# Expert layers: five split buffers, slabs split before the gather, zeros written during the layer before, and 8 KB weight rows with gate and up products of 256 columns

## The reference, cut to what matters

```python
def moe_ffn(x, w_router, b_router, w_gate, w_up, w_down):
    ...
    s = jax.nn.sigmoid((xt @ w_router).astype(jnp.float32))
    biased = s + b_router.astype(jnp.float32)
    grp_score = lax.top_k(biased.reshape(n, N_EXPERT_GROUPS, EXPERTS_PER_GROUP), TOP_K)[0].sum(-1)
    grp = jnp.argmax(grp_score, axis=-1)
    ...
    h = jax.nn.silu(jnp.einsum('nd,edf->nef', xt, w_gate)) * jnp.einsum('nd,edf->nef', xt, w_up)
    h = h * gate[:, :, None].astype(h.dtype)
    return jnp.einsum('nef,efd->nd', h, w_down).reshape(B, S, D)
```

## Time and profile before

| | us |
|---|---|
| median of three runs | 2281.39 (2280.94 to 2286.85) |
| profiled execution, its own time | 2280.86 |
| its span in the trace | 2279.1 |
| first expert layer, from its first POOL instruction to the last down product's start | 1159.80 to 1442.96 |
| second expert layer, likewise | 1962.79 to 2245.17 |
| PE, DVE, ACT, POOL busy over the span | 90%, 61%, 42%, 7% |

### The profile page before, as it was taken

How to read it: one execution, slowest core, us unless ns; L and a number is a source line. 1 busy time by engine, 2 the same in 40 slices (tenths; PEclk the granted TensorE clock), 3 DMA queues, 4 the chain that set the end, 5 groups by cost and what they waited for, 6 DMA issues and landing times. The chain is left out here.

```text
span 2279.1 us, 29889 instructions
## 1 busy us (share of the span) xinstructions
PE 2046.0 (90%) x11912; PEld 1732.2 (76%) x11912; DVE 1383.8 (61%) x1962; ACT 949.9 (42%) x1399; POOL 151.4 (7%) x209
## 2 busy tenths in 40 slices
PE   5999988969999898999979999699968887799995
PEld 5888878869999786776758888478957666688784
DVE  7864545545555454533468999745036675689896
ACT  5653335221000001623447777421125552477773
POOL 3442000000000000000020001000000000010010
PEclk9999998989999999999989999899879999799998
DMA  7433112214232223221249999432420002199993
GB/s 212 109 73 95 56 56 94 74 36 123 76 110 76 73 75 98 79 89 38 74 150 363 388 390 383 169 89 93 117 76 1 1 1 73 40 363 386 386 385 145
DMA packets 162200, 325.53 MB, mean 143 GB/s; under 512 B 30176, under 2 KB 98464, under 8 KB 161936
## 3 DMA queue, kind: packets, MB, share of 16 engines
q1 hardware_dynamic: 133872, 282.92, 35.4%
q0 software_dynamic: 11792, 32.33, 4.4%
q10 hardware_dynamic: 16400, 8.39, 1.5%
HBM read 299.41 MB, written 18.94 MB: 140 GB/s over the span
## 5 line engine op out<-in xcount | busy, mean ns | idle before, releaser
L2277 PE MATMUL ps<-m_ws,m_xbT 128*128 128x512 f32 x1344 | 317.8, 392 | 1.6 <-DVE m_ws L2515 1.6
L2277 PEld LDWEIGHTS ps<-m_ws,m_xbT 128*128 128x128 f32 x1344 | 254.0, 189 | 54.9 <-DVE m_ws L2515 1.8
L2515 DVE TENSOR_TENSOR m_ws<-ring,m_ws 128x2048 fp32r<-128x2048 f32 x112 | 255.8, 2290 | 38.2 <-ACT m_ws L2355 31.6
L1630 PE MATMUL ps<-ffT,ff_ws 128*128 128x264 f32 (+1 forms) x1056 | 241.7, 324 | 4.4 <-DVE ff_ws L433 4.4
L2355 ACT CAST m_ws<-ring 128x2048 fp32r<-128x2048 f32 x112 | 213.2, 1909 | 74.5 <-PE ps L2277 38.6
L1630 PEld LDWEIGHTS ps<-ffT,ff_ws 128*128 128x128 f32 x1056 | 176.9, 190 | 20.2 <-DVE ff_ws L433 4.5
L2319 PE MATMUL ps<-m_ws,m_hT 128*128 128x512 f32 x672 | 170.6, 404 | 0.0
L1630 PE MATMUL ps<-ffT_lo,ff_ws 128*128 128x264 f32 (+1 forms) x528 | 170.3, 323 | 0.0
L2319 PEld LDWEIGHTS ps<-m_ws,m_hT 128*128 128x128 f32 x672 | 124.4, 192 | 24.7
L2512 DVE TENSOR_TENSOR m_ws<-ring,m_ws 128x2048 fp32r<-128x2048 f32 x56 | 128.2, 2290 | 12.9 <-ACT m_ws L2353 12.3
L460 PE MATMUL ps<-fd_ws,fd_xs 128*128 128x512 f32 x528 | 121.9, 394 | 6.7 <-DVE fd_xs L433 6.7
(11 more groups left out here) (540 smaller groups left out, 4295.0 us busy)
## 6 DMA issues: line engine op xcount, KB each, us to landing
ring<-in_moe_w_gate SPq DMA_DIRECT2D x112, 512.0 KB
ring<-in_moe_w_up SPq DMA_DIRECT2D x112, 512.0 KB
ring<-in_moe_w_down SPq DMA_DIRECT2D x56, 1024.0 KB
ring<-in_w_up SPq DMA_DIRECT2D x22, 1024.0 KB
ring<-in_w_in SPq DMA_DIRECT2D x16, 1024.0 KB
ring<-in_gla_w_in SPq DMA_DIRECT2D x12, 1024.0 KB
ring<-in_w_down SPq DMA_DIRECT2D x11, 1024.0 KB
ring<-in_nsa_w_in SPq DMA_DIRECT2D x10, 1024.0 KB
```

The source lines that it names most:

```text
L1630: ins = nc.tensor.matmul(ps[:, bank, 0:b - a], w[j][:, k, s * P:(s + 1) * P], x[l][:, k, a:b], start=(k == 0 and j == l), stop=(k == KD - ...
L2277: ins = nc.tensor.matmul(ps[:, it % 2, :], xbT[:, blk % 2, a, 4 * half + k, :].bitcast(F32R), v[b][:, k, :], start=(half == 0 and k == 0 a ...
L2515: ins = V.tensor_tensor(o, x.rearrange("p (j k w) -> p j k w", k=4, j=2), x0, ALU.subtract)
```

## The change

1. `SPLITS` becomes 5. Room for the fifth buffer is made by laying `rows` over `xT`. `rh` and `rl` move to buffers 3 and 4.
2. Slab 2 is therefore rounded by ACT ahead of the copies to `xbT`, and DVE splits slab 0 ahead of the router's ranking, slabs 1 and 2 where slabs 0 and 1 were, and 3 and 4 where 2 and 3 were.
3. POOL writes the zeros at the end of `gla_project`, from `xT`, for blocks 2 to 6 of `x_slots` (before: 0 to 6), `y_slots` and `g_slots`; ACT waits for them at the start of the expert layer.
4. A gate slab holds all of one expert's gate weights and an up slab all of its up weights. Each of the 128 partitions receives one run of 8 KB (before: two runs of 4 KB from two tensors). Down slabs are laid out as (p k) and not (k p), which is also a run of 8 KB; the transposes of `hb` take every second column to match. Gate and up become 48 matmuls with 256 columns, first all of gate, then all of up.

```diff
-SPLITS = 4
+SPLITS = 5
...
                 if down:
                     units[u][2] = self.W.add((slab_view(2, D), lambda expert=expert: expert("moe_w_down_2")
-                                              .rearrange("o (k p) w -> p (o k) w", p=P)))
+                                              .rearrange("o (p k) w -> p (o k) w", p=P)))
                     continue
-                for half in range(2):
-                    units[u][half] = self.W.add(*[
-                        (lambda s, j=j: s[:, 1024 * j:1024 * j + 1024],
-                         lambda name=name, half=half, expert=expert: expert(name)
-                         .rearrange("o (p k) w -> p o (k w)", p=P)[:, 0, 1024 * half:1024 * half + 1024])
-                        for j, name in enumerate(("moe_w_gate_2", "moe_w_up_2"))])
+                for j, name in enumerate(("moe_w_gate_2", "moe_w_up_2")):
+                    units[u][j] = self.W.add((lambda s: s, lambda name=name, expert=expert: expert(name)
+                                              .rearrange("o (p k) w -> p o (k w)", p=P)[:, 0, :]))
         return units
...
+                pool.wait_ge(o_done, N)
+                zero = m["xT"][:, 2:4].rearrange("p a c -> p (a c)")
+                nc.gpsimd.memset(m["xT"][:, 2:6], 0.0).then_inc(zeroed, 1)
+                pool.wait_ge(zeroed, 1)
+                for blk in range(2, NB):
+                    pool.dma_start(self.x_slots[P * blk:P * (blk + 1), :], zero).then_inc(self.zeros_in, 16)
+                pool.dma_start(self.y_slots[P * (NB - 2):P * NB, :].rearrange("(b p) d -> p b d", p=P),
+                               m["xT"][:, 2:6].rearrange("p (b a) c -> p b (a c)", b=2)).then_inc(self.zeros_in, 16)
+                pool.dma_start(self.g_slots.rearrange("(b p) e -> p b e", p=P), zero[:, 0:NB * EG].rearrange("p (b e) -> p b e", e=EG))\
+                    .then_inc(self.zeros_in, 16)
...
-            rows = sb(ctx, tag + "_rows", [P, TT, D])
+            rows = xT[:].rearrange("p k c -> p (k c)").rearrange("p (t d) -> p t d", t=TT)
...
-            rh, rl = (ws[:, 2 + y].rearrange("p a (t c) -> p (a t) c", t=2) for y in range(2))
+            rh, rl = (ws[:, 3 + y].rearrange("p a (t c) -> p (a t) c", t=2) for y in range(2))
...
-            n_sent = 16 * (2 * TT + (NB + 3 if first else 0))
+            n_sent = 16 * 2 * TT
...
                         for half in range(2):
                             q = at[units[it][half]]
                             pe.wait_ge(lo_done, q + 1)
-                            v = [slab_view(4, 512)(part(q, y)) for y in range(2)]
-                            for k in range(4):
-                                if it == 0:
-                                    pe.wait_ge(xp_out, 4 * half + k + 1)
+                            v = [slab_view(KD, 256)(part(q, y)) for y in range(2)]
+                            for k in range(KD):
+                                if it == 0 and half == 0:
+                                    pe.wait_ge(xp_out, k + 1)
                                 for a, b in ((0, 0), (0, 1), (1, 0)):
-                                    ins = nc.tensor.matmul(ps[:, it % 2, :], xbT[:, blk % 2, a, 4 * half + k, :].bitcast(F32R),
-                                                           v[b][:, k, :], start=(half == 0 and k == 0 and a == b),
-                                                           stop=(half == 1 and k == 3 and a == 1))
+                                    ins = nc.tensor.matmul(ps[:, it % 2, 256 * half:256 * half + 256], xbT[:, blk % 2, a, k, :].bitcast(F32R),
+                                                           v[b][:, k, :], start=(k == 0 and a == b), stop=(k == KD - 1 and a == 1))
                             ins.then_inc(slab_read, 1)
...
                         for k in range(2):
-                            ins = nc.tensor.transpose(ps[:, 2, P * k:P * (k + 1)], hb[:, u % 2, P * k:P * (k + 1)], self.ident[:])
+                            y = hb[:, u % 2].rearrange("p (q k) -> p k q", k=2)[:, k, :]
+                            ins = nc.tensor.transpose(ps[:, 2, P * k:P * (k + 1)], y, self.ident[:])
                         ins.then_inc(t_done, 1)
...
+                if first:
+                    act.wait_ge(self.zeros_in, 16 * NB)
...
                     x = W.slot(slabs[q])
-                    if down[q]:
-                        nc.scalar.copy(part(q, 0), x).then_inc(hi_done, 1)
-                    else:
-                        nc.scalar.copy(part(q, 0).rearrange("p (k j w) -> p j k w", k=4, j=2),
-                                       x.rearrange("p (j k w) -> p j k w", k=4, j=2)).then_inc(hi_done, 1)
+                    nc.scalar.copy(part(q, 0), x).then_inc(hi_done, 1)
...
                 nc.scalar.activation(s[:], ps[:, 4, 0:TT * NE], ACT.Sigmoid).then_inc(s_out, 1)
                 round_x(2)
                 round_x(3)
+                hi(2)
                 act.preload_act_table(ACT.Silu)
                 for k in range(KD):
                     act.wait_ge(xp_done, k + 1)
                     nc.scalar.copy(xbT[:, :, :, k, :].rearrange("p b a c -> p a b c").bitcast(F32R),
                                    ps[:, xbank[k], :].rearrange("p (a b c) -> p a b c", a=2, b=2)).then_inc(xp_out, 1)
-                hi(2)
                 hi(3)
+                hi(4)
...
-                if first:
-                    nc.gpsimd.memset(xb[:, 0, :], 0.0).then_inc(zeroed, 1)
-                    pool.wait_ge(zeroed, 1)
-                    for blk in range(NB):
-                        pool.dma_start(self.x_slots[P * blk:P * (blk + 1), :], xb[:, 0, 0:D]).then_inc(sent, 16)
-                    for blk in range(LAST, NB):
-                        pool.dma_start(self.y_slots[P * blk:P * (blk + 1), :], xb[:, 0, 0:D]).then_inc(sent, 16)
-                    pool.dma_start(self.g_slots.rearrange("(b p) e -> p b e", p=P), xb[:, 0, 0:NB * EG].rearrange("p (b e) -> p b e", e=EG))\
-                        .then_inc(sent, 16)
-                    pool.wait_ge(sent, 16 * (NB + 3))
                 pool.wait_ge(slot_done, 1)
...
                     x = W.slot(slabs[q])
-                    if down[q]:
-                        ins = V.tensor_tensor(part(q, 1), x, ws[:, q % SPLITS, 0], ALU.subtract)
-                    else:
-                        o, x0 = (y.rearrange("p (k j w) -> p j k w", k=4, j=2) for y in (part(q, 1), ws[:, q % SPLITS, 0]))
-                        ins = V.tensor_tensor(o, x.rearrange("p (j k w) -> p j k w", k=4, j=2), x0, ALU.subtract)
+                    ins = V.tensor_tensor(part(q, 1), x, ws[:, q % SPLITS, 0], ALU.subtract)
...
                 rest_x(0)
                 rest_x(1)
+                lo(0)
                 dve.wait_ge(loaded, 16 * len(loads))
                 dve.wait_ge(s_out, 1)
...
                     V.tensor_scalar(onehot[:, t].bitcast(F32R), slots, slotf[:, t:t + 1], None, ALU.is_equal).then_inc(hot, 1)
                 V.tensor_copy(slot[:], slotf[:]).then_inc(slot_done, 1)
-                lo(0)
                 lo(1)
+                lo(2)
...
                 V.tensor_copy(gid[:], gidf[:]).then_inc(gid_done, 1)
-                lo(2)
                 lo(3)
+                lo(4)
```

More of the change, by code:

```diff
@@ L1818, in gla_project @@
             ybank = (0, 4, 6, 2)
-            centred = self.sem("gl_centred")
+            centred, zeroed = self.sems("gl", "centred", "zeroed")
+            self.zeros_in = self.sem("zeros_in")
             self.n_ln += 1
@@ L2196, in moe_stage @@
             NQ = len(slabs)
-            down = [n in {u[2] for u in units} for n in slabs]
             block = ctx.enter_context(nc.Block())
```

## The result

The changed kernel took **2296.32 us** (median of 6 runs, 2295.77 to 2298.45), the kernel before 2282.64 us in the same comparison: ratio 1.006, 95% interval 1.0047 to 1.0073. It is 0.6% slower.

A forecast was written before the change was run, and what follows sets the result against it. PE was taken to bound the kernel, with DMA close behind. The terms 14.7 + 3.2 - 7 + 6 = +16.9 on the profiled 2280.86 gave 2297.8; with the median 0.5 above, 2298 us, range 2279 to 2314.

The forecast's parts named there:

- Passes: Gate and up in all 56 units: 48 passes of 256 columns cost 10.9 ns more per pair, +14.7 us.
- row 4's pace: Attention layer's passes of the same kind, 118.8 ns each, taken as the pace of the short gate and up passes.
- Head: Start of both expert layers: earlier split delays the ranking by 0.7 us, unit 0 waits for copies; +3.2 us, 0 to +6.
- gate waits for the last copy, +2.2: Unit 0: all of gate needs all eight copies to `xbT`, so the unit ends at 1203.5 where it ended at 1201.25.
- Zeros: POOL's zero transfers leave layer 0's head, seven moving to the end of the GLA layer, where they are covered: 0.
- Tail: End of each expert layer: the fifth buffer and longer units remove two thirds of 10.5 us, -7 us, ends -10.5 and -3.
- Block loads: Six loads of blocks 4 to 6, against 8 KB rows: +1 us each, +6 us, from -6.2 to +24.
- each of the 8 + 8 rows waits for one weight row: Block loads: on each engine token and gate rows alternate with weight rows; 8 KB rows add 2.6 us per load.
- Rival A: Starved loads: 8 KB packets delay each of the six block loads by 3 to 4 us; up to 2315, chance 0.15.
- Rival B: Blocks 4 to 6 and tail: PE asks for 3% less bandwidth, so DMA keeps up; 2281, chance 0.25.
- Rival C: Gate and up: short passes cost no more in pairs, 113.3 ns each; 2283, or 2270 with part of B; chance 0.10.
- Rival D: Weight queues: rows still move in packets of 4 KB, loads gain 0.26 us each; 2290, chance 0.15.

The follow-up runs named there:

- before_again: The kernel before, unchanged, profiled again on the same chip as the other kernels of its batch: ratio 0.9999 to the kernel before.
- old_slabs: The changed kernel without its slab layout (4 KB runs, 512-column products as before; fifth buffer, early splits and zeros stay): ratio 0.9955 to the kernel before.
- old_slabs_four: old_slabs with four split buffers in place of five: ratio 0.9998 to the kernel before.
- short_4k: old_slabs with 22 of 24 gate and up passes doubled into products of 256 columns, still on 4 KB runs: ratio 1.0 to the kernel before.
- both: old_slabs with a separate semaphore for the gates, so that PE waits for a block's tokens alone: ratio 0.9932 to the kernel before, median 2264.01 us.
- gates_apart: The changed kernel with a separate semaphore for the gates; PE waits for a block's tokens alone, only DVE for gates: ratio 0.9989 to the kernel before.
- after_again: The changed kernel, unchanged, profiled again on the same chip as before_again: ratio 1.0078 to the kernel before.

## Why the prediction was right, and where its terms were not

The side and the time were right: 2298 us and 0.7% slower were forecast, 2296.3 and 0.6% measured. Its own terms sum to +16.9; the first profiles differ by 15.3, those of one chip by 18.4. The side rests on the mechanism: short passes and later gates, less the tail. That the size agrees so well is luck, since four terms were off, by +4.3 (passes), -3.0 (head), -5.0 (tail) and +8.3 (loads), and 3.1 us lie outside the expert layers (19.0 + 0.2 - 12.0 + 14.3 - 3.1 = 18.4):

- **Passes: +14.7 forecast, +19.0 found** (56 units x 0.34). The step that failed is the choice of row 4's pace, 118.8 ns, over the upper end of 120.0 from the earlier trace rows. The passes came at 120 ns, and the strided transposes add 0.02 us a unit. An isolated gap of N/2.4 + 2.5 ns (the Trainium skill, "TensorE: Matmul & The Clock Gate", Back-to-back issue gap) would make 109.2 ns of them; the rows do not agree with it for these operands.
- **Head: +3.2 forecast, +0.2 found** beyond the longer passes of units 0 and 1. The ranking starts later as said, but by 0.44 us a layer instead of 0.7. The step "gate waits for the last copy, +2.2" failed: the late copies of the earlier trace rows belonged to that execution and not to the kernel. In before_again they end 3.6 us sooner after the start of unit 0, in time for gate. The 1.3 us of unit 1's wait for a split, which the step takes off again, is gone with them: before_again has no such wait.
- **Zeros: 0, right.** Neither pair of profiles shows a cost in the first layer's head: it grows by 0.46 us, and the second layer's, which never wrote zeros, by 0.42. (Their cover was sized a little wrong: 3.7 MB at 315 GB/s are 12 us and not 13.)
- **Tail: -7 forecast, -12.0 found** beyond one longer unit in each, past the end of -10.5. The fifth buffer alone gives 7.4 (old_slabs against old_slabs_four), which is what was forecast; in short_4k the longer units give another 3.1, or 3.7 beyond the longer unit itself, which the step named but did not price.
- **Block loads: +6 forecast, +14.3 found,** the term that decides, within its range of -6.2 to +24. Direction and place were right: blocks 4 to 6, and the gates behind the tokens. Of the 14.3, 9.6 are longer waits (4.4 to 14.0 us, 1.6 a load where +1 was taken), and the other 4.7 are what the step left out: three times the clock fell behind such a wait, 1.55 us each. Of the mechanism a part holds: "each of the 8 + 8 rows waits for one weight row" on all engines would have spread the gates evenly, and they are not spread evenly (below).

Rival A (loads delayed by 3 to 4 us each, +21) is off in this term by about as much as the forecast: in the second pair of profiles the gates of blocks 4 to 6 land 1.9 us later in the mean. Rival B's mechanism shows in short_4k (load waits from 5.5 to 2.7 us); the new layout undoes it. Rival C falls with 120 ns a pass. Rival D, rows that still move in packets of 4 KB, falls: the trace has packets of 8192 bytes, of 309 ns in the median, where 4096 bytes took 159.

So the fifth buffer's gain was there and was paid away: in the old layout it is worth 10 us, and 5 more come from a wait that covered too much (both).

## What to carry to other kernels

A semaphore should cover only what the waiting instruction reads: two transfers of very different urgency on one count make the small one's queueing the big one's. Where a bound engine has a close second, price what an edit does to the second's latency, not only to its bandwidth: a row of 8 KB took 309 ns where two of 4 KB take 318, and still the layout with long rows cost 14 to 18 us over short_4k, as long as PE waited for the gates; with the gates apart (gates_apart) nothing of it was left. And a change made of several parts should be timed part by part, since here one part paid for the others.

## What was unexpected of the hardware

- **Long rows made the load uneven: most of it came sooner, the last rows later.** In the trace's record of single packets, the load of block 5 in layer 0: with 4 KB rows (before_again) the last token row starts 2.1 us after the median one, and the last gate row 1.6 after the median gate row. With 8 KB rows (after_again) it is 4.0 and 6.0 us; half the gate rows have gone by 0.6 us after the median token row, and the last 16 of 128 take 1.8 us by themselves. In the changed kernel's first profile, at the load of block 4, the last ten gate rows start mostly in pairs, 0.31 us from pair to pair, which is the time of one 8 KB packet. By the Trainium skill ("DMA: Bandwidth & Descriptors", Queues, rings and completion order) an engine goes round its queues packet by packet, which agrees with that spacing; why some rows are left so far behind when weight rows are long, no run here shows.
- **A long wait costs more than itself.** In the thirteen profiles PE waits for a block's load 0.4 to 2.01 us at a time in many units, and each of them takes 0.24 to 0.30 us more than the wait, at 2.4 GHz throughout. Behind the nine waits of 2.29 to 3.44 us the unit took 1.8 us more than the wait, a part of it at 1.2 GHz. The length of one wait does not decide it alone: in the first profile of before the clock fell in unit 1 behind 1.30 us, which followed 16 products of 4 columns (1.84 us), and in a tail of old_slabs_four behind 1.93 us.
